# Pooling mix of a two-layer block: products on features without the inverse deviation, its factor and the shift applied where the products leave the bank

## The reference

```python
def rms_norm(x, g):
    y = x * lax.rsqrt(jnp.mean(x * x, axis=-1, keepdims=True) + EPS)
    return y * g
...
# layer 1; h is the state after layer 0's feed-forward part
xn = rms_norm(h, norm_mix_g[1]) * (1 + sc1) + sh1
# pool_mix: per group g of 256 channels, window w in (2, 4, 8, 16)
y = window_mean(xn, w) - xn
y = einsum('bngc,gcd->bngd', y, w_pool) * pool_scale
h = h + g1 * y
hn = rms_norm(h, norm_ffn_g[1]) * (1 + sc2) + sh2
h = h + g2 * (silu(hn @ w1) * (hn @ w3)) @ w2
```

## Time and profile before

| | us |
|---|---|
| time, median of 3 runs | 1174.77 |
| lowest and highest of them | 1172.77, 1175.81 |
| profiled execution, time | 1177.08 |
| profiled execution, span | 1175.3 |
| TensorE busy in the span | 1132.1 (96%) |
| VectorE busy | 822.7 (70%) |
| ScalarE busy | 587.4 (50%) |
| GpSimd busy | 88.0 (7%) |
| mean granted TensorE clock | 0.984 of full |

### The profile page before, as it was taken

How to read it: one execution, slowest core, us unless ns; L and a number is a source line. 1 busy time by engine, 2 the same in 40 slices (tenths; PEclk the granted TensorE clock), 3 DMA queues, 4 the chain that set the end, 5 groups by cost and what they waited for, 6 DMA issues and landing times.

```text
span 1175.3 us, 23850 instructions
## 1 busy us (share of the span) xinstructions
PE 1132.1 (96%) x10189; PEld 1069.5 (91%) x10189; DVE 822.7 (70%) x1493; ACT 587.4 (50%) x1072; POOL 88.0 (7%) x109
## 2 busy tenths in 40 slices
PE   8889889999998999999999999999999999999998
PEld 2776889999997999999989889879999999999998
DVE  6887569888885776645766788878554667677553
ACT  2545554455445545554456557653224545656332
POOL 0001000000011000011000111104500002000000
PEclk9899989999998999999999999999999999999999
DMA  9964369988881567550742422322123554855520
GB/s 390 396 221 149 129 233 357 358 309 333 330 346 72 215 256 279 182 179 11 288 164 88 144 86 96 108 72 73 39 73 131 178 194 164 341 200 192 197 78 14
DMA packets 32219, 225.34 MB, mean 192 GB/s; under 512 B 3569, under 2 KB 4721, under 8 KB 5105
## 3 DMA queue, kind: packets, MB, share of 16 engines
q1 hardware_dynamic: 30530, 221.21, 50.6%
q10 hardware_dynamic: 1584, 2.62, 0.7%
HBM read 222.76 MB, written 1.05 MB: 190 GB/s over the span
## 4 chain that ended last, share of the span: by engine, by line
PE 86%; DVE 7%; ACT 5%; DMA 1%; issue 1%; POOL 0%; DVEq 0%; POOLq 0%; ACTq 0%
PE bank L573 23%; PE bank L575 22%; PE bank L574 22%; DVE sb_wlo L1970 2%; PE bank L1091 2%; ACT sb_whi L1427 2%; DMA sb_ring<-in_ada 1%; PE bank L592 1%; PE bank L1113 1%; PE bank L601 1%; PE bank L1082 1%; PE bank L1279 1%; PE bank L1297 1%; PE bank L1293 1%; PE bank L664 1%
## 5 line engine op out<-in xcount | busy, mean ns | idle before, releaser
L573 PE MATMUL bank<-sb_xh,sb_whi 128*128 128x256 f32 x1480 | 417.9, 282 | 3.3 <-DVE sb_wlo L1970 2.2
L575 PE MATMUL bank<-sb_xh,sb_wlo 128*128 128x256 f32 x1480 | 410.4, 277 | 0.0
L574 PE MATMUL bank<-sb_xl,sb_whi 128*128 128x256 f32 x1480 | 410.4, 277 | 0.0
L1970 DVE TENSOR_TENSOR sb_wlo<-sb_ring,sb_whi 128x1024 fp32r<-128x1024 f32 (+1 forms) x197 | 239.6, 1221 | 124.6 <-ACT sb_whi L1427 124.2
L573 PEld LDWEIGHTS bank<-sb_xh,sb_whi 128*128 128x128 f32 x1480 | 278.7, 188 | 11.3 <-issue 7.8
L574 PEld LDWEIGHTS bank<-sb_xl,sb_whi 128*128 128x128 f32 x1480 | 278.6, 188 | 0.1
L575 PEld LDWEIGHTS bank<-sb_xh,sb_wlo 128*128 128x128 f32 x1480 | 278.2, 188 | 0.0
L1427 ACT ACTIVATE sb_whi<-sb_ring 128x1024 fp32r<-128x1024 f32 (+1 forms) x197 | 206.9, 1053 | 99.4 <-PE bank L575 84.2
L1970 DVE TENSOR_TENSOR sb_wlo<-sb_more,sb_whi 128x1024 fp32r<-128x1024 f32 x108 | 131.1, 1223 | 61.4 <-ACT sb_whi L1427 61.4
L573 PE MATMUL bank<-sb_hh,sb_whi 128*128 128x256 f32 x608 | 168.4, 277 | 0.0
L574 PE MATMUL bank<-sb_hl,sb_whi 128*128 128x256 f32 x608 | 167.8, 276 | 0.0
(11 more groups left out here) (400 smaller groups left out, 1843.1 us busy)
## 6 DMA issues: line engine op xcount, KB each, us to landing
sb_more<-in_w SPq DMA_DIRECT2D x34, 1024.0 KB, 6.0
sb_ring<-in_w SPq DMA_DIRECT2D x32, 1024.0 KB, 5.7
sb_ring<-in_adaT SPq DMA_DIRECT2D x23, 1024.0 KB, 7.4
sb_ring<-in_f SPq DMA_DIRECT2D x22, 1024.0 KB, 4.9
sb_more<-in_adaT SPq DMA_DIRECT2D x21, 1024.0 KB, 8.2
sb_ring<-in_gn SPq DMA_DIRECT2D x8, 1024.0 KB, 4.9
sb_ring<-in_gd SPq DMA_DIRECT2D x8, 1024.0 KB, 4.9
sb_ring<-in_up SPq DMA_DIRECT2D x8, 1024.0 KB, 8.3
```

Of the source, the lines that this page charges most:

```text
L573: te.matmul(out, wh, rh, start=start, stop=False, skip_group_check=skip)
L574: te.matmul(out, wh, rl, start=False, stop=False, skip_group_check=skip)
L575: return te.matmul(out, wl, rh, start=False, stop=stop, skip_group_check=skip)
L1970: ve.tensor_tensor(lo, x, hi.bitcast(F32), ALU.subtract).then_inc(*lo_dve.up(n))
```

## The change

Instead of normalizing `h` before the channel products, the kernel multiplies plain `h * scale` (without the inverse deviation) by the channel weights. The split parts `xh`, `xl` of `mix1` are written output by output during the down products: ScalarE writes `xh` from `h` right after each square, VectorE writes `xl` (`lower_scaled`) one output later. The shift vector, split as `shh` and `shl`, goes through the channel weights in products of its own (`shift_through`, two of 12 matmuls, its column repeated over the 128 columns of the stationary side), and ScalarE copies their results to `sw` (`shift_out`). VectorE then takes each `z` out of its bank as z * (inverse deviation of the token) + `sw`. `spread("mix1")`, `apply("mix1")`, `upper("mix1")` and the idle products of that norm are gone. TensorE's order is: shift product 0, mean square, shift product 1, `z`. VectorE's two splits of the units ahead are placed one before the residuals of the pool products and one behind the third. In the norm `ffn1`, GpSimd sums squares 1 to 4 only, and TensorE multiplies squares 5 and 6 by the column of ones itself.

```diff
+ADDED = {"ffn1": 4}
...
+        sw = junk[:, :].rearrange("p (g c) -> p g c", g=4)
...
 def mean_square_rest(norm):
-                P.wait_ge(*pool.at("sum", norm, KT - 2))
-                for t in range(2):
-                    te.matmul(ps[:, t:t + 1], sq[:, 0, t * 128:(t + 1) * 128], ones[:, 0:1], start=t == 0, stop=False, skip_group_check=True)
-                idle(2 * (norm != "mlp2"))
+                added = ADDED.get(norm, KT - 2)
+                P.wait_ge(*pool.at("sum", norm, added))
+                for k in (0, *range(added + 1, KT - 1)):
+                    if k:
+                        P.wait_ge(*act.at("sq", norm, k))
+                    for t in range(2):
+                        te.matmul(ps[:, t:t + 1], sq[:, k, t * 128:(t + 1) * 128], ones[:, 0:1], start=(k, t) == (0, 0), stop=False, skip_group_check=True)
+                idle(2 * (norm not in ("mix1", "mlp2")))
...
 TensorE, after the down products of layer 0
+            def shift_through(i, u):
+
+                _, hi, lo = unit_of(u)
+                P.wait_ge(*lo_done(u))
+                P.wait_ge(*dve.at("shl"))
+                ps = take(RO, ("sw", i), (act, ("sw", i)))
+                for e in range(2):
+                    g = 2 * i + e
+                    for c in range(2):
+                        o = e * 512 + c * T
+                        x, y = columns(shh[:, 2 * g + c:2 * g + c + 1]), columns(shl[:, 2 * g + c:2 * g + c + 1])
+                        end = mm3(ps[:, e * T:(e + 1) * T], x, y, hi[:, o:o + T], lo[:, o:o + T], c == 0, c == 1)
+                end.then_inc(*pe.up(("sw", i)))
...
+            shift_through(0, pair[0])
+            mean_square_rest("mix1")
+            shift_through(1, pair[1])
             for g in range(4):
...
-                    ps = take(RG, ("z", g, t), (act, ("z", g, t)))
+                    ps = take(RG, ("z", g, t), (dve, ("z", g, t)))
...
 ScalarE, in swiglu and behind it
+                if layer == 0:
+                    A.wait_ge(*dve.at("ada", 1, 7))
+                    sc.activation(shh[:, :], mods[:, 1, 0:8], ACT.Copy).then_inc(*act.up("shh"))
...
                     square(after, j, h, dve.at("h", after, j), ("ms", norm))
+                    if layer == 0:
+                        if j == 0:
+                            A.wait_ge(*dve.at("scl3"))
+                            A.wait_ge(*pe.at("x", "ffn0"))
+                        sc.activation(xh[:, j, :], h[:, j, :], ACT.Copy, scale=scl[:, 3, j:j + 1]).then_inc(*act.up(("xh", "mix1", j)))
...
+            shift_out(0)
             deviation("mix1")
-            upper("mix1", mods[:, 1, 0:8], xh, ("x", "ffn0"))
...
+            split([early.pop(0)])
+            shift_out(1)
+            split([early.pop(0)])
...
 VectorE, in swiglu and behind it
+            def lower_scaled(k):
+                V.wait_ge(*dve.at("scl3"))
+                V.wait_ge(*act.at("xh", "mix1", k))
+                ve.scalar_tensor_tensor(xl[:, k, :], h[:, k, :], scl[:, 3, k:k + 1], xh[:, k, :].bitcast(F32), ALU.mult, ALU.subtract).then_inc(*dve.up(("mix1", k)))
...
                     residual(after, j, ("down", layer), mods[:, layer, 40 + j:41 + j])
+                    if layer == 0 and j > 0:
+                        lower_scaled(j - 1)
+                if layer == 0:
+                    lower_scaled(KT - 1)
...
-            apply("mix1", h, scl[:, 3, :], mods[:, 1, 0:8], xh, xl)
...
-            split([early.pop(0), early.pop(0)])
+            V.wait_ge(*dve.at("rs", "mix1"))
+            for g in range(4):
+                V.wait_ge(*act.at("sw", g // 2))
+                for t in range(2):
+                    V.wait_ge(*pe.at("z", g, t))
+                    ve.scalar_tensor_tensor(z8[:, 2 * g + t, :], ps_of(("z", g, t))[:, 0:T], dev[:, NORMS.index("mix1"), t:t + 1], sw[:, g, :],
+                                            ALU.mult, ALU.add).then_inc(*dve.up(("z", g, t)))
+            split([early.pop(0)])
             c = F.raw("poolm")
             for j in range(8):
                 V.wait_ge(*dve.at("gcol"))
                 residual("ffn1", j, "pool", gcol[:, j:j + 1])
+                if j == 2:
+                    split([early.pop(0)])
...
 GpSimd, in sums(norm)
-                for k in range(1, KT - 1):
+                for k in range(1, ADDED.get(norm, KT - 2) + 1):
```

More of the change, by code:

```diff
@@ L375, in program @@
         gcol = sb("gcol", [128, 8])
+        shh = sb("shh", [128, 8], F32R)
+        shl = sb("shl", [128, 8], F32R)
         warm = sb("warm", [128, 1])
@@ L918, in swiglu @@
                         n += 1
-                if layer == 0:
-                    mean_square_rest(after)
-                else:
+                if layer == 1:
                     mean_squares_last()
                 pe.note(("hid", layer))
-                if layer == 0:
-                    spread(after)
             swiglu(0, "ffn0", "mix1")
-            for g in range(4):
[L931 to L936, removed]
+            def shift_through(i, u):
[10 more added lines that the diff above has]
+                end.then_inc(*pe.up(("sw", i)))
+            pair = [F.take("poolw", 1)[0]]
+            F.done(pair[0])
+            pair += [F.take("poolw", 1)[0]]
+            F.early(3)
+            F.done(pair[1])
+            shift_through(0, pair[0])
+            mean_square_rest("mix1")
+            shift_through(1, pair[1])
+            for g in range(4):
+                _, hi, lo = unit_of(pair[g // 2])
                 for t in range(2):
-                    ps = take(RG, ("z", g, t), (act, ("z", g, t)))
+                    ps = take(RG, ("z", g, t), (dve, ("z", g, t)))
                     q = slice(t * 128, (t + 1) * 128)
@@ L943, in tensor_program @@
                         end = mm3(ps[:, 0:T], xh[:, 2 * g + c, q], xl[:, 2 * g + c, q], hi[:, o:o + T], lo[:, o:o + T], c == 0, c == 1)
-                    end.then_inc(*pe.up(("z", g, t), ("unit", u)) if g % 2 and t else pe.up(("z", g, t)))
-                if g % 2:
-                    F.done(u)
+                    end.then_inc(*pe.up(("z", g, t), ("unit", pair[g // 2])) if g % 2 and t else pe.up(("z", g, t)))
             pe.note(("x", "mix1"))
@@ L953, in tensor_program @@
                 for t in range(2):
-                    P.wait_ge(*act.at("z", j // 2, t))
+                    P.wait_ge(*dve.at("z", j // 2, t))
                     o = (j // 2 * 2 + t) * T
@@ L1630, in scalar_program, with shift_out @@
             swiglu(0, "ffn0", "mix1", "layer0", ahead)
-            deviation("mix1")
-            upper("mix1", mods[:, 1, 0:8], xh, ("x", "ffn0"))
[L1633 to L1642, removed]
+            weights("poolw", 1)
+            weights("poolw", 1)
+            early = F.early(3)
+            def shift_out(i):
+                A.wait_ge(*pe.at("sw", i))
+                sc.activation(flat(sw[:, 2 * i:2 * i + 2, :]), ps_of(("sw", i))[:, :], ACT.Copy).then_inc(*act.up(("sw", i)))
+            shift_out(0)
+            deviation("mix1")
+            split([early.pop(0)])
+            shift_out(1)
+            split([early.pop(0)])
             c = F.raw("poolm")
@@ L2186, in swiglu @@
                 m3 = dve.now()
+                if layer == 0:
+                    V.wait_ge(*dve.at("ada", 1, 15))
+                    scaled(3, C("nm", 8, 16), mods[:, 1, 8:16])
+                    dve.note("scl3")
+                    V.wait_ge(*act.at("shh"))
+                    ve.tensor_tensor(shl[:, :], mods[:, 1, 0:8], shh[:, :].bitcast(F32), ALU.subtract).then_inc(*dve.up("shl"))
                 n = 0
@@ L2200, in vector_program @@
             swiglu(0, "ffn0", "mix1", 2, ahead)
-            V.wait_ge(*dve.now())
-            scaled(3, C("nm", 8, 16), mods[:, 1, 8:16])
+            inverse_deviation("mix1")
             ve.tensor_tensor(gcol[:, :], mods[:, 1, 16:24], C("ps"), ALU.mult).then_inc(*dve.up("gcol"))
             scaled(4, C("nf", 8, 16), mods[:, 1, 32:40])
-            inverse_deviation("mix1")
-            apply("mix1", h, scl[:, 3, :], mods[:, 1, 0:8], xh, xl)
-            for g in range(0, 4, 2):
-                weights("poolw", 1)
+            weights("poolw", 1)
+            weights("poolw", 1)
             early = F.early(3)
-            split([early.pop(0), early.pop(0)])
+            V.wait_ge(*dve.at("rs", "mix1"))
[6 more added lines that the diff above has]
+            split([early.pop(0)])
             c = F.raw("poolm")
```

## The result

The changed kernel takes 1185.15 us (median of 6 runs, 1181.92 to 1204.25) against 1175.29 us for the kernel before in the same session (6 runs, 1170.86 to 1176.02). The ratio is 1.0078, with a 95% interval of 1.0059 to 1.0098: 6.9 to 11.5 us slower, where 8 us less were forecast.

What follows compares the result with a forecast made beforehand. TensorE, with 86% of the chain of waits, bounds the kernel. About 6.9 us gained up to the pool products' end, 0.6 from sums, 0.7 from clock: 1174.77 - 8.2 = 1166.6 us, range 1164.2 to 1170.7.

Steps and rivals of the forecast that it cites:

- Load added to the down products: Down products: each output adds a 0.48 us VectorE operation and a 0.4 us ScalarE copy, covered by idle time; cost nothing.
- what follows at 373.08 is the same code in both kernels: After the row factor of `ffn1`: nothing changes, so only the 28.5 us stretch from 344.54 was costed.
- the slower one: Rival, down products, 284 to 344.5: VectorE becomes the bound at 3.1 us added per output; 1178 us and more; chance 0.04.
- Item 1: Norm `mix1`: `xh` and `xl` made during the down products, off TensorE's path; last `xl` near 346.6.
- Item 2: Shift products: 24 matmuls of 0.113 us, 2.7 us on TensorE's path; 5.0 at the low clock.
- Items 3 and 4: Mean square of `mix1`, 0.7 us; then 48 `z` matmuls of 0.113 us, 5.4 us, ending at 353.4.
- its 2.2 us of cover: In `z`: the inverse-deviation factor, expected at about 347.3, may come as late as 349.5 without stalling `z`.
- Item 5: Pool products: 7.0 us, to 360.4; the bank wait is hidden by 0.1 to 0.5 us.
- Item 6: Squares of `ffn1`: fourth GpSimd sum, slowed beside the second VectorE split, ends at 360.7; mean square at 363.1.
- Item 7: From mean square of `ffn1` to row factor: 1.73 us at full clock instead of 2.42, ready at 364.85.
- one of my rivals, with a chance of 0.17: Low clock in the shortened stretch: `z` or shift +1.4 us, `spread` +0.7, both +2.1; 1168 to 1169 us; chance 0.17.
- The base of the sum: Stretch from last down product to row factor of `ffn1` in the profiled execution before: 373.08 - 344.54 = 28.5 us.

Runs made afterwards that it cites:

- b_pad: Kernel before with `shh` and `shl` declared behind `gcol` but never used, later tiles 64 bytes further: 1190.76 us, ratio 1.0122 to before.
- a_place: Changed kernel with `shh` and `shl` declared behind `z8`, so all other tiles keep the addresses of before: 1171.34 us, ratio 0.9960 to before.
- a_256: Changed kernel with 192 bytes more behind `shl`, later tiles 256 bytes further than in the kernel before: 1169.31 us, ratio 0.9944 to before.
- b_hh: Kernel before with `hh`, `hl`, the extra weight slots and `z8` alone 64 bytes further: 1182.63 us, ratio 1.0061 to before.
- a_again: Changed kernel unaltered, run again for a trace at the full granted clock: 1185.99 us, ratio 1.0080 to before.
- a_even: Changed kernel with 64 bytes more behind `shl`, later tiles 128 bytes further than in the kernel before: 1181.66 us, ratio 1.0039 to before.
- a_noidle: Changed kernel with `shh` and `shl` behind `z8` and without the two idle products between squares 6 and 7 of `ffn1`: 1169.01 us, ratio 0.9937 to before.
- a_nosq: Changed kernel with GpSimd's six sums back in `ffn1` (`ADDED = {}`): 1187.05 us, ratio 1.0095 to before.
- b_again: Kernel before unaltered, run again for a second trace: 1176.01 us, ratio 1.0004 to before.
- b_sq: Kernel before with the squares part alone: GpSimd sums squares 1 to 4 in `ffn1`, TensorE takes the others: 1173.06 us, ratio 0.9982 to before.

## Why the prediction was wrong, point by point

*The step that failed* is the costing of the change part by part: it gave no cost at all to the two declarations of `shh` and `shl`, took the down products at their old pace (its heading "Load added to the down products" ends with nothing), and took "what follows at 373.08 is the same code in both kernels" for "the same time". Every tile declared behind them moved by 64 bytes: `hh`, `hl`, `ah`, `al`, and in the second block `onh`, `mxh`, `odh`, `hh2` and their lower halves. `b_pad` shows that this alone costs 14.5 us, `a_place` and `a_256` that without it the change gains 4.2 and 6.5 us. The six `gap` declarations stood in the code of the kernel before, and the prediction does not ask what they are for. None of my rivals was this one; the slower one looked for a wait on VectorE in the down products of layer 0, and there was none. Its time, 1178 and more, was met by another mechanism: 1.00 clock, no idle time, and 119 instead of 113 ns. Its place was right in part, since the down products of layers 0 and 1 together hold 7.1 of the 14.5 us (`b_hh`) and the rest lies in later stages.

The Trainium skill speaks to this. The page "SBUF — State Buffer", section "Who interferes with whom", gives TensorE two independent read ports, one for the moving operand and one for the weight load, and the page "TensorE: Matmul & The Clock Gate", section "Step-by-step: what each phase is for", says that loading the next weights does not take read bandwidth from the running matmul. Neither section speaks of addresses. If the two reads never met, one would expect the distance between the tiles to cost nothing, and that expectation fails here: 355 or 336 records in 40 us with nothing changed but where tiles lie. The measurement decides; that it is these two reads that meet is not shown.

*The stretch itself*, in microseconds from the end of the down products (344.54 in the prediction, 344.97 in `a_again`):

| station | forecast | measured |
|---|---|---|
| `z` ends | 8.9 | 9.3 |
| fourth sum ends | 16.2 | 16.8 |
| mean square of `ffn1` ready | 18.6 | 19.6 |
| first tile of `apply` (forecast: row factor) | 20.3 | 22.3; 21.4 without low clock (`a_even`) |

*Item 1, right.* Nothing of TensorE waits for `xh` or `xl`; it goes from the down products into the shift without a gap.

*Item 2, right.* The first 12 shift matmuls take 11 steps in 346.22 - 344.97 = 1.25 us, 0.114 each. The 12 behind the mean square start at 347.14 and take 1.49 us up to `z`, 0.13 more than the first.

*Items 3 and 4, right in kind, 0.4 short.* `z` runs at (354.17 - 348.63)/47 = 0.118, not 0.113, and the last squares take 0.45, not 0.35. I had priced `z` by the step of the down products, though its own steps stood in the same trace: 0.119 from 350.77 to 351.72, and 0.113 only behind the low clock, 13 steps between these two lines of the trace of before:

```profile
358.07 0.28 PE L574 MATMUL bank<-sb_wlo,sb_xh 128*128 128x256 f32 x1
...
359.54 0.28 PE L575 MATMUL bank<-sb_whi,sb_xl 128*128 128x256 f32 x1
```

The reciprocal ends at 347.78, 0.5 later than I put it and inside its 2.2 us of cover; VectorE's first outlet waits for `z`, not for the factor.

*Item 5, right, with the products 0.4 longer.* No bank held TensorE; the pool products run from 354.28 to 361.66, 7.4 us where I had 7.0.

*Item 6, right mechanism, two terms small.* The second split took 1.75 us where the first took 1.22, and the two sums beside it 2.39 together, where a sum in a series took 0.87: both engines were slowed, as in the pair of the trace of before. That one shuts the other out for its whole length these records do not show, since both grew, by 0.5 and by 0.65. TensorE's 12 records for three squares took 1.50 where I had 1.02. The two idle products took 0.97, as forecast, and lie wholly on the path; `a_noidle` takes them out.

*Item 7, half right.* In `a_even` and `a_noidle` `spread` ran at the full clock; in `a_again` the low one came before it, 1.82 for the four idles. It was one of my rivals, with a chance of 0.17, which is small beside what the traces have: in `a_place`, `a_256` and `a_nosq` it comes there too, which makes four of the seven traces in the new order (`a_even`, `a_noidle` and the first one of the changed kernel do not). It costs 0.9 us, 22.3 against 21.4.

*The base of the sum was too high.* The trace of before had two low stretches of the clock among the 28.7 us; 2.1 us of the gain that I worked out were those. The 5.2 us without low clock are the 8.2 forecast, less 2.1, less 1.1 for the terms above (21.4 instead of 20.3), and 0.2 more because the stretch is 28.7 us by the marks used here and was 28.5 by mine. Some low clock comes to both versions, so the times may gain a little more or less: 4.2 and 6.5 us were measured.

*The load added to the down products* cost nothing: in `a_256` they have 356 records, as before, with VectorE busy for 35.41 of 40 us instead of 33.75.

## What to carry to other kernels

A declaration is a change, and an unexplained gap between tiles is a reason to ask. Before an edit is timed, compare the addresses of every tile that TensorE reads, and put new small tiles where they move nothing, or pad to the period that the products show (here 256 bytes); time the bare declarations as a version of their own when a gain is missing and no wait is to be found. And count the low stretches of the clock in the profiled execution before its times are taken for a base.

## What the runs showed of the hardware that was not expected

TensorE's pace in a stream of float32 products, each with its own weight load of 128x128 and a moving tile of 128x256, depends on the distance between the addresses of the two tiles (moving less stationary) in the down products: 113 ns at 192 modulo 256 bytes, 117 at 64, 119 at 0 and 128. Over the kernel this is worth 14.5 us (1.2%) when the tiles behind `gcol` move, and 37.7 us (3.2%) when the weights move against all. The pace at distance 0 was the same, 336 records, with the tiles at 128 and at 192 modulo 256; the other distances were tried with the weights at one place only. In `z` the moving side is `whi` and the stationary side `xh`, a distance of 64. It ran at 118 ns in `a_again` and `b_again`, but at 113 in the end of the trace of before, so it proves nothing for the distance; with `b_sq` from 975 to 990 it shows that 113 and 118 ns both occur at one and the same distance, for a reason not found here. That the two reads collide in the memory is my reading and is not shown. Distances between tiles of one stream that are no multiple of 64 were not tried.
